# Every second U product of the gathered rows moved from VectorE to GpSimd and ScalarE in two attention stages, and 11 more row pairs placed there

## What is computed

```python
def one(xb):                                     # 128 tokens
    ...                                          # scores, top-16 per head: eidx, gate
    u_rows = expert_u[eidx]                      # 8 x 16 rows of 1024 per token
    act = gelu(einsum('thkd,td->thk', u_rows, xb))
    w = gate * act
    return einsum('thk,thkd->td', w, expert_v[eidx])
```

## Time and profile before

| | |
|---|---|
| median of 3 runs | 5053.72 us (5047.71 to 5055.49) |
| the profiled execution | 5064.18 us |
| its span | 5062.4 us |
| DVE busy | 3119.5 us, 62% |
| PE busy | 3650.2 us, 72% |
| ACT busy | 1526.2 us, 30% |
| POOL busy | 1340.6 us, 26% |
| attention stage of chunk 1 | about 1437 to 1776 us |
| attention stage of chunk 2 | about 2384 to 2767 us |
| tail | about 3541 us to the end |

### The profile page before, as it was taken

One profiled execution on the slowest core, in us unless ns is written; L12 is line 12 of the kernel. 1 busy time (PEld: TensorE's weight loads), 2 busy tenths in 40 slices (PEclk: granted clock), 3 DMA queues, 4 the chain that ended last, 5 costly groups with the idle time before them and its releaser, 6 DMA issues. The chain is left out here.

```text
span 5062.4 us, 44057 instructions
## 1 busy us (share of the span) xinstructions
PE 3650.2 (72%) x13408; PEld 2059.8 (41%) x13408; DVE 3119.5 (62%) x6957; ACT 1526.2 (30%) x3824; POOL 1340.6 (26%) x1167
## 2 busy tenths in 40 slices
PE   6965689696766576686665875757777777777776
PEld 4543466574433343342444764424322222222221
DVE  4145210315777877677888657768766666666664
ACT  3111010312324432142444433221333333333333
POOL 0000000002222223223222323224444444444443
PEclk9955559898987788898887887879999999999999
DMA  2011314248866687888556999769999999999997
GB/s 80 35 19 1 3 51 150 80 162 307 353 246 221 241 354 275 343 346 340 198 206 240 399 372 387 316 251 368 408 419 417 416 410 415 412 411 407 408 411 314
DMA packets 281661, 1416.06 MB, mean 280 GB/s; under 512 B 44226, under 2 KB 85666, under 8 KB 144322
## 3 DMA queue, kind: packets, MB, share of 16 engines
q0 software_dynamic: 159344, 1129.94, 56.2%
q1 hardware_dynamic: 121698, 283.19, 16.5%
q10 hardware_dynamic: 384, 0.13, 0.0%
HBM read 1369.87 MB, written 40.93 MB: 279 GB/s over the span
## 5 line engine op out<-in xcount | busy, mean ns | idle before, releaser
L807 POOL DMA_INDIRECT arena<-in_uv,arena x1056 | 1272.1, 1205 | 2486.6 <-DVE arena L918 1591.5
L908 DVE CUSTOM_DVE_ANT_0 arena<-arena 128x1024 f32<-128x1024 f32 x1056 | 1288.3, 1221 | 499.8 <-DMA arena<-in_uv,arena 469.9
L1024 PE MATMUL ps<-arena 128*128 128x512 f32 (+1 forms) x2320 | 1108.6, 624 | 417.2 <-ACT arena L993 417.2
L1091 PE MATMUL ps<-arena 128*128 128x256 f32 (+2 forms) x3456 | 1125.3, 487 | 222.4 <-DMA arena<-in_w_stat 54.3
L1091 PEld LDWEIGHTS ps<-arena 128*128 128x128 f32 x3456 | 693.9, 204 | 618.5 <-issue 448.9
L1024 PEld LDWEIGHTS ps<-arena 128*128 128x128 f32 (+1 forms) x2320 | 423.3, 191 | 1101.9 <-ACT arena L993 638.6
L918 DVE SCALAR_TENSOR_TENSOR arena<-arena 128x1024 f32<-128x1024 f32 x476 | 608.6, 1279 | 35.8 <-ACT arena L983 35.8
L974 ACT ACTIVATE arena<-arena 128x2 f32<-128x2 f32 x528 | 107.2, 203 | 1723.6 <-DVE arena L908 1723.2
L983 ACT ACTIVATE arena<-arena 128x1 f32<-128x1 f32 x1056 | 253.4, 287 | 17.8 <-ACT arena L974 0.7
L813 POOL DMA_DIRECT2D arena<-in_iota x1 | 0.7, 704 | 933.0 <-POOLq L1972 933.0
L974 ACT ACT_TABLE_LOAD x157 | 201.4, 1283 | 4.7 <-issue 1.9
(11 more groups left out here) (251 smaller groups left out, 3758.6 us busy)
## 6 DMA issues: line engine op xcount, KB each, us to landing
arena<-in_w_stat SPq DMA_DIRECT2D x216, 512.0 KB, 7.3
arena<-in_cache_k SPq DMA_DIRECT2D x64, 512.0 KB, 11.0
arena<-in_cache_v SPq DMA_DIRECT2D x64, 512.0 KB, 12.0
arena<-in_w_mov SPq DMA_DIRECT2D x14, 2048.0 KB, 13.0
arena<-in_uv,arena POOLq DMA_INDIRECT x1056, 13.1
arena<-in_x SPq DMA_DIRECT2D x16, 512.0 KB, 4.6
arena<-scr_s POOLq DMA_DIRECT2D x64, 128.0 KB, 12.9
scr_s<-arena SPq DMA_DIRECT2D x16, 384.0 KB, 12.2
```

Of the source, the lines that this page charges most:

```text
L807: pool.indirect_dma_start(ring[s % RING], None, dr["uv"], bass.IndirectOffsetOnAxis(ap=idx[:, g % 4, j:j + 1], axis=0)).then_inc(row_in[s ...
L908: nc.vector.tensor_tensor_reduce(ring[s % RING][:, 0:D], ring[s % RING][:, 0:D], h2r[:, b % 2, :], 1.0, 0.0, ALU.mult, ALU.add, act_in[:, ...
L1024: last = nc.tensor.matmul(ps[0:m, 4 * (b % 2) + c, :], diag[:, n % 4, 0:m], ring[s % RING][:, D + 512 * c:D + 512 * (c + 1)], start=start, ...
L1091: last = nc.tensor.matmul(ps[:, bank, 0:w], wbuf[m % NWB][:, kc * P:(kc + 1) * P], moving[:, kc, :], start=(kc == 0), stop=(kc == KC - 1))
```

## The change

It has three parts.

1. `PAIR_PLAN` places 32 instead of 27 pairs in the attention stage of chunk 1 and 34 instead of 28 in that of chunk 2. The tail gets 11 fewer, 279 instead of 290.
2. For each of these 66 pairs (`POOL_PAIRS`) DVE no longer does the second dot. POOL multiplies the U half by `h2` in place (`u_product`), and ACT copies the product onto itself while it sums it (`u_total`).
3. The waits follow: `dots` no longer counts these slots, and a load of `h2` into a buffer waits for POOL's products too.

The product of pair p+1 stands in POOL's step p, ahead of that step's two gathers and behind those of step p-1. The sum of pair p is the first thing in ACT's step p.

```diff
-                     (7, 14, 9, 27, 0, 14, 7, 18),
-                     (8, 15, 10, 28, 40, 15, 8, 18))
+                     (7, 14, 9, 32, 0, 14, 7, 18),
+                     (8, 15, 10, 34, 40, 15, 8, 18))
...
+        AT_ATT = STAGES.index("att")
+        POOL_PAIRS = [p for c in range(1, len(CHUNKS)) for p in range(PAIRS_BEFORE[c] + sum(PAIR_PLAN[c][:AT_ATT]),
+                                                                        PAIRS_BEFORE[c] + sum(PAIR_PLAN[c][:AT_ATT + 1]))]
+
+        def u_pool_before(p):
+            return len([k for k in POOL_PAIRS if k < p])
+
+        def dots_before(p):
+            return 2 * p - u_pool_before(p)
...
-                pool.wait_ge(dots, 2 * end_pair(b - 2))
+                pool.wait_ge(dots, dots_before(end_pair(b - 2)))
+                if u_pool_before(end_pair(b - 2)):
+                    pool.wait_ge(u_pool, u_pool_before(end_pair(b - 2)))
...
+        def u_product(pool, p):
+
+            s = 2 * p + 1
+            b = head_block(s // TOPK)
+            loaded, n = h2_sem(b)
+            pool.wait_ge(loaded, n)
+            pool.wait_ge(row_in[s % RING], 16 * (s // RING + 1))
+            nc.gpsimd.tensor_tensor(ring[s % RING][:, 0:D], ring[s % RING][:, 0:D], h2r[:, b % 2, :], ALU.mult).then_inc(u_pool, 1)
+
+        def u_total(act, p):
+            k = (2 * p + 1) % RING
+            act.wait_ge(u_pool, u_pool_before(p) + 1)
+            nc.scalar.activation(ring[k][:, 0:D], ring[k][:, 0:D], ACT.Copy, accum_out=act_in[:, k:k + 1]).then_inc(u_sum, 1)
+            act.wait_ge(u_sum, u_pool_before(p) + 1)
...
+            if p + 1 in POOL_PAIRS:
+                u_product(pool, p + 1)
             for s in (range(AHEAD) if p == -1 else range(2 * p + AHEAD, 2 * p + AHEAD + 2)):
...
-                if p < PAIRS:
+                if p < PAIRS and not (q and p in POOL_PAIRS):
                     u_dot(dve, 2 * p + q)
...
-                act.wait_ge(dots, 2 * p + 2)
+                if p in POOL_PAIRS:
+                    u_total(act, p)
+                act.wait_ge(dots, dots_before(p + 1))
```

More of the change, by code:

```diff
@@ L719, in hybrid_step @@
         names = ("pc_in", "tk_v", "tk_done", "ex_d", "gt_v", "dots", "gelu_d", "wgt_d", "diag_d", "v_dve", "v_pe",
-                 "acc_out", "y_sq", "y_ms", "y_rt", "y_rc", "y_done")
+                 "acc_out", "u_pool", "u_sum", "y_sq", "y_ms", "y_rt", "y_rc", "y_done")
         (pc_in, tk_v, tk_done, ex_d, gt_v, dots, gelu_d, wgt_d, diag_d, v_dve, v_pe,
-         acc_out, y_sq, y_ms, y_rt, y_rc, y_done) = (sem(n) for n in names)
+         acc_out, u_pool, u_sum, y_sq, y_ms, y_rt, y_rc, y_done) = (sem(n) for n in names)
         row_in = [sem(f"row_in{k}") for k in range(RING)]
```

## The result

| | before | changed |
|---|---|---|
| median of 4 runs | 5054.36 us | 5137.91 us (5135.69 to 5145.03) |
| ratio of the runs | | 1.0171, 95% interval 1.0153 to 1.0188 |
| profiled execution, its span | 5064.18, 5062.4 us | 5145.03, 5143.3 us |

The change costs 1.7%, some 84 us. The forecast was 12 us in the other direction, and the time lies above the top of the range (5085).

The account below looks back on a forecast made before the run. Transfers were taken to bound the tail, DVE's fixed order the two attention stages. Tail -57.1 and DVE -12.8 gave -70 us; products holding DVE added 58: -12 us, 5042 us. Range 4985 to 5085 us, likeliest case 5023 to 5057.

Parts of the forecast that it names:

- What bounds each stage: Tail paced by gathers, 57.1 us for 11 pairs; attention stages set by DVE's order, nearly a microsecond per microsecond.
- The open cost of the product: POOL's product beside DVE in the attention stages: holds DVE 0.78 and 0.98 us each in the mean, 58 us together.
- let DVE give way, and POOL get in only when DVE leaves its two-operand run: Attention stages: POOL's product can't slip into short gaps of DVE's run; 58 us lost, net -12 us, chance 0.38.
- the gather of 7.57 us: A POOL wait in the trace before, taken to show DVE's two-operand runs keeping POOL out.
- Rival 1: Attention stages: POOL's product takes the first gap and holds DVE's two-operand instructions; 88 us, net +18, 5072 us; chance 0.30.
- what I listed as hiding no product: DVE in the attention stages: `probabilities` (line 1541, 0.75 us, and what precedes it), dots and `v_add`s don't hide a product.
- -70 us if nothing collides: Whole kernel without interference: DVE's changes save 8.1 us in chunk 1 and 4.7 in chunk 2, the tail 57.1.
- ACT's sum costs nothing: ACT ahead of the GELU: 66 sums of 1.24 us, 40 and 42 us, covered by its 75.6 us wait.
- The product's gathers come late without harm: POOL's queue in the attention stages: gathers come 2.2 us later, rows are fetched three steps ahead, so no cost.
- ACT's copy of the probabilities: Queued on ACT behind the sums, PE waits for it; only holding it up could bring ACT's extra work to the end.
- Rival 3: Attention stages don't follow DVE: spared time goes into waiting for PE or ACT; -7 us, about 5047 us; chance 0.05.
- Rival 2: Attention stages: DVE is hardly held by POOL's product; gain 57 to 70 us, 4984 to 4997 us; chance 0.27.

Follow-up runs that it names:

- plan only: The kernel before with 32 and 34 pairs in the two attention stages and all dots left on DVE: 5078.55 us, ratio 1.0046.
- product of 1 column: The changed kernel with POOL multiplying 1 column instead of 1024, all waits, queues, ACT's sum and pair placement kept: 5039.02 us, ratio 0.9968.

## Why the prediction was wrong

**What bounds each stage: right.** The tail is paced by gathers and gave 59 us for 11 pairs (57.1 forecast). The attention stages follow DVE when it gets more to do: 56 and 47 us more busy time made them 57 and 63 us longer. When it gets less, they follow in part: from the kernel with the plan only to the one with a product of 1 column, DVE's busy time in the two stages falls by 71 us and their length by 50.

**The open cost of the product: wrong, by 41 us of the time.** This miss alone turns the sign. I forecast 0.88 us of DVE time a product and 58 us in all. It is 1.7 us by the lengthened instructions, 114 us in all; 99 us of it are in the time (changed kernel against the 1-column product). The failing step is "let DVE give way, and POOL get in only when DVE leaves its two-operand run". POOL's products hardly wait, as their median of 2352 ns (ten of 66 take over 2.4 us, one 3.18) and idle time of 7.4 us show; it is DVE that waits. The row that I leaned on, the gather of 7.57 us, shows that POOL can be kept out, and says nothing of who is kept out when POOL is already in. Rival 1 had the mechanism and 88 us. It was still short. The product takes 2.41 us in the mean, not 2.2. I let only two-operand instructions be held, while the TENSOR_SCALAR of 128x16 (line 926) went from 235 to 1762 ns, and in chunk 2 from 234 to 2302. And what I listed as hiding no product leaves out the square of the output and the product of line 1574, which lost 27 and 6 us in the two stages. The rule of the Trainium skill that I weighed (SBUF — State Buffer, Who interferes with whom: the first to issue wins for its whole instruction) fits DVE's side: a 128x2 instruction took 2.46 us beside a product of 2.35. The experiment in which POOL only writes agrees with its two clauses too: free two-operand instructions at 292 and 161 ns, held one-operand ones at 749 and 1340 ns. Two things don't bear it out in full. Who issued first can't be read from the recorded starts: the 128x2 instruction starts 0.09 us ahead of the product that holds it, and a dot of 4.45 us at 1480.61 starts 0.98 us ahead of its product, with POOL in a gather and another transfer's issue until then. And POOL's one-operand instruction holds a two-operand one for 1.1 of its 2.8 us, not for the whole. I gave rival 1 0.30 and should have given it most.

**-70 us if nothing collides: wrong by 56 us.** Without the product's length the kernel is 14 us faster, not 70. This is the larger of the two misses, and would have turned the sign by itself as well. These terms made it up. The plan was to cost 5 us (63 in the stages, 57 back) and costs 25 in the medians: the stages' own share was right to 4 us, 9 more appear in the other stages, and the rest is mostly the 10.5 us by which the trace of before lies above its median. The swap was to save 66 x 1.14 = 75 us and saves 39. Of that, part is visible: two `v_add`s in a row take 2.67 us instead of 1.28 + 1.20, since the second waits until the first has ended (`v_dve`), which is 0.19 x 66 = 13 us; and DVE waits 6.3 and 8.0 us for weights that ACT's sum has delayed (1.1 us and none before). So "ACT's sum costs nothing" was wrong by up to 13 us. These two account for about what the stages lack: in the traces they are 50 us shorter than with the plan only, of 75. The rest lies outside of them, where the code is the same: the kernel with a product of 1 column loses 12 us there, 5 of them in the decoding stage, and why is open.

**What was right besides, and what was not.** The product's gathers come late without harm: no dot waits for its row. ACT's copy of the probabilities was to have cover; in chunk 1 it has not in full. PE waits for it 21.2 us, 24.7 with a product of 1 column, against 12.9 with the plan only and 8.4 before; in chunk 2 it stays at 10 to 11 us. DVE feels little of it: its wait for PE before line 1577 is 1.1 us in chunk 1, and 3.8 in chunk 2. POOL's filling takes 0.85 us per 1024 by the earlier trace rows, not 0.83, which changes none of the sums. Rival 3 (the stage doesn't follow DVE) is out: the wait of line 1511 stayed at 44.6 us. Rival 2 is out by the held means.

**The range.** Its upper end, 5085, took rival 1's price on top of a sum whose other terms had no bounds of their own. With the -70 bounded at even half its size, the top would have been at 5120 or more.

## What to carry to other kernels

Work moved from DVE to POOL is not off DVE's path if POOL reads SBUF: an instruction on 2 elements a lane took 2.46 us instead of 0.16 beside a product of 2.35 us. Before the move, list what DVE has to do in those microseconds and in which form; a product beside reductions out of PSUM held none of them, the same product beside instructions with two SBUF operands cost most of its length. And before filling the time that a swap is meant to free, measure the swap alone: the 11 pairs cost more than they brought even without it (1.0046).

## What the runs showed of the hardware that I had not expected

- POOL's multiply by a constant of 1024 float32 takes 2.87 us in the mean (2.77 at least), longer than its product of two tensors of that size (2.35), yet holds DVE less (444 against 1101 ns on line 1579), because it holds a two-operand instruction only for its first 1.1 us.
- POOL's filling of 2048 2-byte elements takes 1.82 us, 0.89 ns an element, near its 0.85 ns for 4-byte elements.
- A one-column product takes 0.21 us (median), so a POOL product has little fixed cost: (2.35 - 0.21)/1023 is 2.1 ns an element.
- Two `v_add`s in a row onto one accumulator, the second waiting for the first, cost DVE 0.19 us more than the same two with a dot between them.
